# Stream states updated in place in a ring of five rooms, reads of two streams in turn, convolution rows written inside the set-up

## The chip, the core and the metric

One core of a Trainium2 chip runs the whole program. The time is the device time of one execution in microseconds (us), and smaller is better. TensorE (PE) multiplies, VectorE (DVE), ScalarE (ACT) and GpSimd (POOL) compute element by element, SyncE (SP) issues most DMAs. Every engine works through its own list of instructions in order and waits on semaphores.

## What is computed

Two layers, each with a token mixer (layer 0: S5, layer 1: mLSTM) and a convolutional feed-forward net (FFN), run over one prompt of 1024 tokens and over eight running streams of 16 tokens. The change lies at the end of layer 0's FFN and the projection of layer 1 (whose last convolution rows are outputs), and in the mLSTM of the eight streams, which have four heads with a 512 x 512 state matrix each:

```python
num = einsum(sc, v) + a * einsum('bqhk,bhvk->bqhv', q, C)      # read of the old state C
den = sum(sc) + a * einsum('bqhk,bhk->bqh', q, n)
h = num / maximum(abs(den), exp(-m_t))
C_new = decay * C + einsum('blh,blhv,blhk->bhvk', wg, v, k)    # update, an output
n_new = decay * n + einsum('blh,blhk->bhk', wg, k)
xp = concatenate([buf, x]); new_buf = xp[:, -(width - 1):]     # last rows of a convolution, an output
```

All data are float32. Eight streams times four heads are 32 state matrices of 1 MB; each is read once from HBM and written once.

## The kernel before

The program is a row of stages. A stage is a block: each engine runs its part, and the block ends when all five have arrived at its end. `front` ends layer 0 and projects layer 1; it leaves the last convolution rows in two tiles, `tails` (44 tiles of 18 columns) and `m_tails` (16 tiles of 27 columns).

`rows_out` (L1111) then runs twice, once for each tile, as a block of its own: PE turns four tiles at a time into one of four PSUM banks (L1126), DVE copies the bank into `stack` (L1133), SP stores the rows when all are there (L1139) and waits for the store.

`cell_setup` (L2335) makes the masks (POOL, L2374 to L2396), folds the weights and computes the gates' running sums and maxima, most of it in one chain on DVE (L2439 to L2492). ACT serves the chain with four functions (L2425 to L2433), PE with the picking of gate rows at the start (L2410) and turns at the end (L2418).

`mlstm_streams` (L2876) has three blocks. In the first, SP loads (L2945 `nrow`, L2947 `row`, L2951 the inputs x of a head) and each of the four heads is projected (PE, L2515 and L2518), turned into weights, split into a head and a rest (the operands of the updates) and written to HBM by SP (`write`, L2943). POOL loads these back in another layout, 48 rows to a pair of streams: `stack_load` (L2933), 12 DMAs for a head, into `v3` and `k3`, of which there are two each. The order of SP's list is the order in which the lines are written. POOL does the stacking loads of heads 0 and 1 here, those of heads 2 and 3 in the second block.

The second block does the 32 state matrices, one a step, head by head and stream by stream. In a step PE turns the matrix (16 transposes of 128 x 128 into banks 0 to 3, L3100), ACT copies the four banks to `cts` (L3114), PE makes four updates of 128 x 512 into banks 5 and 7 in turn (L3082, contraction over the 48 stacked rows), DVE adds each to the decayed state (L3126), and PE makes four reads (L3088), whose result of 32 rows lies in the PSUM partitions of the stream's pair, `32 * (s // 2)`. A head's first step has one more matmul (L3094). The order of PE's work is written by hand: transposes, two updates, two reads, two updates, two reads. Three rooms of four strips hold states that were loaded (`craw`; the third is made of other tiles), two more (`cnew`) hold new states until they are stored. SP, when a step's updates are done, issues the load for three steps later (L2923 and L2926) and then the store (L3068). DVE waits until the store before last has landed, since it writes into its room.

The third block ends the streams (normaliser, norm, output). After it come the prompt's mLSTM, the down projection and layer 1's FFN, which the change does not touch.

## Time and profile before

| | us |
|---|---|
| median of three timed runs (3935.04 to 3937.03) | 3936.26 |
| time of the profiled execution | 3934.65 |
| its span, first to last instruction | 3932.6 |
| writing out the convolution rows (two blocks) | about 22.7 |
| set-up | 55.5 |
| streams, first block | 64.2 |
| streams, second block (32 steps) | 240.0 |

PE is busy 89% of the span, DVE 49%, ACT 29%, POOL 13%. A timeline row gives the start, the length and the engine, then the line, operation and tiles with the number of instructions merged, and in brackets how long the engine was idle before it and who released it. "SPq" and "POOLq" rows are DMAs being issued, not moved. A float32 matmul appears as two records on PE, except a transpose and one with rounded operands. PEclk is the share of the full PE clock that was granted: 0.50 is 1.2 GHz and 1.00 is 2.4 GHz.

### The profile page before, as it was taken

To read this page: it belongs to the slowest core of one execution; us is meant where nothing else is said; L and a number is where in the kernel's file an instruction comes from. 1 tells how busy PE (TensorE), PEld (TensorE's weight loads), DVE (VectorE), ACT (ScalarE), POOL (GpSimd) and SP (SyncE) were. 2 spreads that over 40 slices of the span, in tenths; PEclk is the share of its full clock that TensorE was granted. 3 is DMA by queue.
4 is the path that set the end of the run, shared out by engine and by line. 5 is a ranking of instruction groups with operands and counts; after the bars stand their busy time and mean duration, and the time that the engine had idled before them with its cause. 6 is when DMAs were issued, how large, how long until landed. Compare 5 with 4: busy or idle time off the path is not lost. (4 is left out here: it accounts for less than half of the span.)

```text
span 3932.6 us, 53760 instructions
## 1 busy us (share of the span) xinstructions
PE 3504.0 (89%) x20489; PEld 3252.7 (83%) x20489; DVE 1917.5 (49%) x2968; ACT 1135.5 (29%) x1865; POOL 509.5 (13%) x765
## 2 busy tenths in 40 slices
PE   5549999999999989999279969997995999999997
PEld 4449989999999989999144468887995999999996
DVE  8933554445445462222533346664655444454455
ACT  5233343332232232222122212222112423322321
POOL 2240111000000120000011032221001100000000
PEclk7669999999999999999589979999997999999998
DMA  3544431111111223332289722221112111111112
GB/s 78 141 119 136 132 96 43 41 41 44 44 43 43 71 87 121 107 105 93 41 233 309 257 77 84 76 76 70 43 64 76 44 44 41 41 44 44 44 38 101
DMA packets 366173, 337.08 MB, mean 86 GB/s; under 512 B 42758, under 2 KB 293894, under 8 KB 365826
## 3 DMA queue, kind: packets, MB, share of 16 engines
q1 hardware_dynamic: 345332, 289.11, 24.1%
q0 software_dynamic: 13456, 37.61, 3.4%
q10 hardware_dynamic: 7176, 7.35, 0.6%
q8 instruction: 157, 2.57, 0.3%
q14 instruction: 52, 0.43, 0.0%
HBM read 231.12 MB, written 100.53 MB: 84 GB/s over the span
## 5 line engine op out<-in xcount | busy, mean ns | idle before, releaser
L1583 PE MATMUL pair<-x_head,w_head 128*128 128x384 f32 x1488 | 506.5, 340 | 54.3 <-DVE w_rest L840 30.9
L1583 PE MATMUL pair<-x_rest,w_head 128*128 128x384 f32 x1488 | 503.5, 338 | 0.0
L1583 PE MATMUL pair<-x_head,w_rest 128*128 128x384 f32 x1488 | 503.0, 338 | 0.0
L840 DVE TENSOR_TENSOR w_rest<-w_raw,w_head 128x1024 fp32r<-128x1024 f32 x228 | 291.5, 1279 | 416.6 <-ACT w_head L836 416.5
L836 ACT ACTIVATE w_head<-w_raw 128x1024 fp32r<-128x1024 f32 x228 | 242.4, 1063 | 688.6 <-PE pair L856 167.0
L1238 PE MATMUL pair<-x_head,w_head 128*128 128x384 f32 x1056 | 354.0, 335 | 10.3 <-DVE w_rest L840 8.2
L1238 PE MATMUL pair<-x_rest,w_head 128*128 128x384 f32 x1056 | 353.5, 335 | 0.0
L1238 PE MATMUL pair<-x_head,w_rest 128*128 128x384 f32 x1056 | 353.4, 335 | 0.0
L1583 PEld LDWEIGHTS pair<-x_head,w_head 128*128 128x128 f32 x1488 | 284.2, 191 | 59.2 <-issue 51.2
L1328 DVE SCALAR_TENSOR_TENSOR cv<-u,par,cv 128x1024 f32<-128x1024 f32 x88 | 112.8, 1281 | 357.7 <-ACT u L1294 357.7
L1583 PEld LDWEIGHTS pair<-x_rest,w_head 128*128 128x128 f32 x1488 | 284.3, 191 | 0.0
L1583 PEld LDWEIGHTS pair<-x_head,w_rest 128*128 128x128 f32 x1488 | 284.1, 191 | 0.0
L1851 DVE SCALAR_TENSOR_TENSOR cv<-u,par,cv 128x1024 f32<-128x1024 f32 x88 | 112.8, 1281 | 341.1 <-ACT u L1792 341.1
L1238 PEld LDWEIGHTS pair<-x_head,w_head 128*128 128x128 f32 x1056 | 198.7, 188 | 11.3 <-issue 9.1
L1238 PEld LDWEIGHTS pair<-x_rest,w_head 128*128 128x128 f32 x1056 | 198.8, 188 | 0.0
L1238 PEld LDWEIGHTS pair<-x_head,w_rest 128*128 128x128 f32 x1056 | 198.8, 188 | 0.0
L1753 PE MATMUL pair<-a_head,w_head 128*128 128x384 f32 x528 | 179.0, 339 | 2.1 <-DVE f L1882 1.0
L1259 PE MATMUL pair<-a_head,w_head 128*128 128x384 f32 x528 | 179.3, 339 | 1.5 <-DVE f L1355 0.4
L1289 ACT ACTIVATE cv<-pair,par 128x384 f32<-128x384 f32 x132 | 88.5, 670 | 314.9 <-PE pair L1238 303.9
L1259 PE MATMUL pair<-a_rest,w_head 128*128 128x384 f32 x528 | 177.5, 336 | 0.0
L1259 PE MATMUL pair<-a_head,w_rest 128*128 128x384 f32 x528 | 177.5, 336 | 0.0
L1753 PE MATMUL pair<-a_head,w_rest 128*128 128x384 f32 x528 | 176.7, 335 | 0.0
(501 smaller groups left out, 6907.8 us busy)
## 6 DMA issues: line engine op xcount, KB each, us to landing
w_raw<-in_ffn_w_up_dram SPq DMA_DIRECT2D x88, 512.0 KB, 3.8
out_dram<-hs SPq DMA_DIRECT2D x64, 512.0 KB, 7.0
w_raw<-in_s_w_glu_dram SPq DMA_DIRECT2D x48, 512.0 KB, 4.0
w_raw<-in_ffn_w_down_dram SPq DMA_DIRECT2D x44, 512.0 KB, 3.7
hs<-in_state_mlstm_C_dram SPq DMA_DIRECT2D x44, 512.0 KB, 5.8
w_raw<-in_mlstm_w_up_dram SPq DMA_DIRECT2D x32, 512.0 KB, 4.5
f<-in_state_mlstm_C_dram SPq DMA_DIRECT2D x40, 256.0 KB
xm_d<-xm SPq DMA_DIRECT2D x16, 576.0 KB, 3.9
```

Source lines behind the costliest of these rows:

```text
L836: act.activation(self.head[slot][:, :], self.raw[slot][:, :], ACT.Copy).then_inc(self.rounded, 1)
L840: dve.tensor_tensor(self.rest[slot][:, :], self.raw[slot][:, :], self.head[slot][:, :].bitcast(F32), ALU.subtract).then_inc(self.split, 1)
L1238: m = pe.matmul(banks[k % 2][c][:, 0:TB], lhs[k % 2][:, P * i:P * i + P], rhs[:, i, TB * c:TB * c + TB], start=(i == 0 and q == 0), stop=( ...
L1259: ins = pe.matmul(banks[m % 2][c][:, 0:TB], lhs[m // 4][:, cols], rhs[s][:, k, TB * c:TB * c + TB], start=(k == 0 and q == 0), stop=(k == ...
L1289: act.activation(cv[g][:, TB * c:TB * c + TB], bk[c][:, 0:TB], ACT.Identity, scale=at(par, t, TAP + H, TAP + H + 1), bias=at(par, t, BIAS, ...
L1328: ins = dve.scalar_tensor_tensor(out=cp, in0=up[:, j:j + SEQ], scalar=tw, in1=cp, op0=ALU.mult, op1=ALU.add)
L1583: m = pe.matmul(out[:, 0:TB], lhs[slot][:, P * k:P * k + P], rhs[:, k, TB * c:TB * c + TB], start=(k == 0 and q == 0), stop=(k == KD - 1 a ...
L1753: ins = pe.matmul(out[:, 0:TB], lhs[m // 4][:, cols], rhs[s][:, k, TB * c:TB * c + TB], start=(k == 0 and q == 0), stop=(k == 1 and q == 2))
L1851: ins = dve.scalar_tensor_tensor(out=cp, in0=up[:, j:j + SEQ], scalar=tw, in1=cp, op0=ALU.mult, op1=ALU.add)
```

## The change

- The two `rows_out` blocks of layer 0 go. `tails` and `m_tails` live on into `cell_setup`, where PE turns them in 15 batches of four into banks 6 and 7, ACT copies each batch into rows of `hs` (not in use yet), and POOL issues the four stores and waits for them.
- First block of the streams: the inputs of head 0 are loaded first and `nrow` last of the early loads; the turn of `nrow` and its copy come after the last head. Five states are loaded ahead, each after a `write`, not three. POOL does the stacking loads of head 0 alone; those of head 1 start with the second block.
- Second block: the streams of a head go in the order 0, 2, 4, 6, 1, 3, 5, 7. DVE writes the new state over the old one, in one of five rooms. SP stores a step's state from its room, then waits for the store of two steps before and loads the state of three steps ahead into that room.
- PE does the reads of two steps together, in turn, after the transposes of the second; the two streams of such a pair lie in different groups of 32 PSUM partitions. The four updates of a step stand together. `cts` exists twice; the second copy is in tiles that hold operands of the writes, so ACT waits for the writes before step 1.
- Two tiles more stay in memory during `front`, and its start address moves by their size.

The diff, cut to what the text speaks of, without its common indent:

```diff
+        for k, (src, tiles, stores) in enumerate(halos):
+            pool.wait_ge(copied, batches.index((k, 0)) + tiles // 4)
+            for dst, r in stores:
+                pool.dma_start(dst, stacks[k][r:r + dst.shape[0], :]).then_inc(halo_out, 16)
+        pool.wait_ge(halo_out, 16 * 4)
...
+        for n, (k, b) in enumerate(batches):
+            src = halos[k][0]
+            rows_ = src.shape[2]
+            if n >= 2:
+                pe.wait_ge(copied, n - 1)
+            for q in range(4):
+                ins = pe.transpose(bank[6 + n % 2][0:rows_, P * q:P * q + P], src[:, 4 * b + q, :], env.ident[:, :])
+            ins.then_inc(halo_turned, 1)
+        pe.wait_ge(copied, len(batches))
...
+        for n, (k, b) in enumerate(batches):
+            act.wait_ge(halo_turned, n + 1)
+            act.activation(stacks[k][:, 4 * P * b:4 * P * b + 4 * P], bank[6 + n % 2][0:halos[k][0].shape[2], :],
+                           ACT.Copy).then_inc(copied, 1)
...
-cnew, cts = [8, 12], 16
-craw = [[strip(4 * b + t) for t in range(HT)] for b in range(2)] + [[flat(t) for t in (*cell.xc, *cell.xm)]]
+ROOMS = 5
+cts = [[strip(16 + k) for k in range(HT)], [flat(t) for t in (*cell.t1, *cell.t2)]]
+craw = [[strip(4 * b + t) for t in range(HT)] for b in range(ROOMS - 1)] + [[flat(t) for t in (*cell.xc, *cell.xm)]]
...
+order = [(h, s) for h in range(HEADS) for s in (0, 2, 4, 6, 1, 3, 5, 7)]
...
-        sp.dma_start(nrow[:, :], n_in[0].rearrange("s h k -> (s h) k")).then_inc(nrow_in, 16)
-        for h in range(HEADS):
-            sp.dma_start(row[:, h, :], rows_d[h, PCH].rearrange("k t -> (k t)").partition_broadcast(P)).then_inc(row_in, 16)
-        for h in range(HEADS):
+        def inputs(h):
             over(sp, projected, h - 1)
             for dst, src in ((cell.xc, xc_d), (cell.xm, xm_d)):
                 sp.dma_start(dst[h % 2][:, :, :], src.rearrange("k p t -> p k t")[:, HT * h:HT * h + HT, last]).then_inc(
                     x_in[h % 2], 16)
-            if h >= 1:
-                c_load(sp, h - 1, h - 1, 0) if h < 3 else None
-            if h >= 2:
-                write(h - 2)
+
+        inputs(0)
+        for h in range(HEADS):
+            sp.dma_start(row[:, h, :], rows_d[h, PCH].rearrange("k t -> (k t)").partition_broadcast(P)).then_inc(row_in, 16)
+        sp.dma_start(nrow[:, :], n_in[0].rearrange("s h k -> (s h) k")).then_inc(nrow_in, 16)
+        inputs(1)
+        inputs(2)
+        write(0)
+        c_load(sp, 0, order[0][1], 0)
+        inputs(3)
+        write(1)
+        c_load(sp, 1, order[1][1], 0)
+        c_load(sp, 2, order[2][1], 0)
         write(2)
         write(3)
-        sp.wait_ge(projected, HEADS)
-        c_load(sp, 2, 2, 0)
+        for n in range(3, ROOMS):
+            c_load(sp, n, order[n][1], 0)
...
-        pe.wait_ge(nrow_in, 16)
-        for k in range(HT):
-            ins = pe.transpose(bank[6][:, SR * k:SR * k + SR], nrow[:, P * k:P * k + P], env.ident[0:SR, 0:SR])
-        ins.then_inc(n_turned, 1)
...
+        pe.wait_ge(nrow_in, 16)
+        for k in range(HT):
+            ins = pe.transpose(bank[6][:, SR * k:SR * k + SR], nrow[:, P * k:P * k + P], env.ident[0:SR, 0:SR])
+        ins.then_inc(n_turned, 1)
...
-            if h >= 2:
-                pool.wait_ge(wrote[h - 2], 64)
+            if h == 2:
+                pool.wait_ge(wrote[0], 64)
                 for n in range(12):
-                    stack_load(pool, h - 2, n)
+                    stack_load(pool, 0, n)
...
-        dve.wait_ge(n_turned, 1)
-        dve.tensor_copy(nt[:, :, :].rearrange("p k r -> p (k r)"), bank[6][:, 0:HT * SR])
...
+        dve.wait_ge(n_turned, 1)
+        dve.tensor_copy(nt[:, :, :].rearrange("p k r -> p (k r)"), bank[6][:, 0:HT * SR])
...
-c_kept = [env.sem(f"c_kept{k}") for k in range(2)]
-order = [(h, s) for h in range(HEADS) for s in range(STREAMS)]
+c_kept = [env.sem(f"c_kept{k}") for k in range(ROOMS)]
...
-        for h in range(2, HEADS):
-            pool.wait_ge(wrote[h % 2], 128)
-            pool.wait_ge(updated, HT * STREAMS * (h - 1))
+        for h in range(1, HEADS):
+            pool.wait_ge(wrote[h % 2], 64 * (h // 2 + 1))
+            if h >= 2:
+                pool.wait_ge(updated, HT * STREAMS * (h - 1))
             for n in range(12):
                 stack_load(pool, h, n)
...
+            b = i % ROOMS
             sp.wait_ge(updated, HT * (i + 1))
-            if i + 3 < SR:
-                nh, ns = order[i + 3]
-                c_load(sp, i % 3, ns, nh)
             for t in range(0, HT, 2):
-                sp.dma_start(c_out[0, s, h, P * t:P * t + 2 * P, :].rearrange("(t p) k -> p t k", p=P),
-                             two_strips(cnew[i % 2] + t)).then_inc(c_kept[i % 2], 16)
-        for p in range(2):
-            sp.wait_ge(c_kept[p], 16 * SR)
+                if b < ROOMS - 1:
+                    sp.dma_start(c_out[0, s, h, P * t:P * t + 2 * P, :].rearrange("(t p) k -> p t k", p=P),
+                                 two_strips(4 * b + t)).then_inc(c_kept[b], 16)
+                else:
+                    for v in (t, t + 1):
+                        sp.dma_start(c_out[0, s, h, P * v:P * v + P, :], craw[b][v]).then_inc(c_kept[b], 16)
+            n = i + ROOMS - 2
+            if i >= 2 and n < SR:
+                sp.wait_ge(c_kept[n % ROOMS], (32 if n % ROOMS < ROOMS - 1 else 64) * (n // ROOMS))
+                c_load(sp, n % ROOMS, order[n][1], order[n][0])
+        for p in range(ROOMS):
+            sp.wait_ge(c_kept[p], (32 if p < ROOMS - 1 else 64) * ((SR - 1 - p) // ROOMS + 1))
...
+        def reads(i, k):
+            h, s = order[i]
+            pair, r = s // 2, s % 2
+            pe.wait_ge(copied, HT * i + k + 1)
+            return pe.matmul(bank[4 + 2 * (h % 2)][32 * pair:32 * pair + 32, :], qz[h][k][:, 64 * pair + 32 * r:64 * pair + 32 * r + 32],
+                             cts[i % 2][k], start=False, stop=(k == HT - 1), skip_group_check=True)
+
         for i, (h, s) in enumerate(order):
-            pair, r, p, num = s // 2, s % 2, i % 2, bank[4 + 2 * (h % 2)]
-
-            def updates(t0):
-                for t in (t0, t0 + 1):
+            pair, r = s // 2, s % 2
+
+            def updates():
+                for t in range(HT):
                     over(pe, updated, HT * i + t - 1)
                     row = slice(64 * r, 64 * r + S3)
                     pe.matmul(bank[5 + 2 * (t % 2)][:, :], v3[h % 2][row, pair, P * t:P * t + P],
                               k3[h % 2][row, pair, :], start=True, stop=True).then_inc(added, 1)
 
-            def reads(k0):
-                for k in (k0, k0 + 1):
-                    pe.wait_ge(copied, HT * i + k + 1)
-                    ins = pe.matmul(num[32 * pair:32 * pair + 32, :], qz[h][k][:, 64 * pair + 32 * r:64 * pair + 32 * r + 32],
-                                    strip(cts + k), start=False, stop=(k == HT - 1), skip_group_check=True)
-                return ins
...
-            pe.wait_ge(c_in[i % 3], (32 if i % 3 < 2 else 64) * (i // 3 + 1))
+            b = i % ROOMS
+            pe.wait_ge(c_in[b], (32 if b < ROOMS - 1 else 64) * (i // ROOMS + 1))
...
-            updates(0)
-            reads(0)
-            updates(2)
-            reads(2).then_inc(inter, 1)
+            if i % 2 == 0:
+                updates()
+            else:
+                for k in range(HT):
+                    for j in (i - 1, i):
+                        ins = reads(j, k)
+                ins.then_inc(inter, 1)
+                updates()
...
+            if i == 1:
+                act.wait_ge(wrote[0], 128)
+                act.wait_ge(wrote[1], 128)
             for k in range(HT):
                 act.wait_ge(turned, HT * i + k + 1)
                 if k == 0:
-                    over(act, inter, i)
-                act.activation(strip(cts + k), bank[k][:, :], ACT.Copy).then_inc(copied, 1)
+                    over(act, inter, i // 2)
+                act.activation(cts[i % 2][k], bank[k][:, :], ACT.Copy).then_inc(copied, 1)
...
-            p = i % 2
-            over(dve, c_kept[p], 32 * (i // 2))
+            room = craw[i % ROOMS]
+            dve.wait_ge(turned, HT * i + HT)
             for t in range(HT):
                 dve.wait_ge(added, HT * i + t + 1)
-                dve.scalar_tensor_tensor(out=strip(cnew[p] + t), in0=craw[i % 3][t],
+                dve.scalar_tensor_tensor(out=room[t], in0=room[t],
...
-        rows_out(env, tails, [(s_fconv[0].rearrange("s h m -> (s h) m"), 0),
-                              (p_fconv[0, 0], STREAMS * (FTAPS - 1))], 2 * FT, (STREAMS + 1) * (FTAPS - 1))
-        rows_out(env, m_tails, [(s_mconv[0].rearrange("s h m -> (s h) m"), 0), (p_mconv[0, 0], STREAMS * MH)],
-                 IT, (STREAMS + 1) * MH)
+        front(env, i, x_head, x_rest, x_res, par, gates, tails, m_tails, xm_d, xc_d, sz_d)
...
+               member, p_m, s_m, hs,
+               ((tails, 2 * FT, [(s_fconv[0].rearrange("s h m -> (s h) m"), 0), (p_fconv[0, 0], STREAMS * (FTAPS - 1))]),
+                (m_tails, IT, [(s_mconv[0].rearrange("s h m -> (s h) m"), 0), (p_mconv[0, 0], STREAMS * MH)])))
+    early.close()
```

PE in the second block. Before, one step from the head's extra matmul on; the `x2` rows are the halves of updates and of reads:

```order
L3094 MATMUL pair<-f,c_sc_331 128x512
L3100 MATMUL pair<-ident,hs 128x128 x16
L3082 MATMUL pair<-k_354,v_352 128x512 x2
L3088 MATMUL pair<-hs 32x512 x2
L3082 MATMUL pair<-k_354,v_352 128x512 x2
L3088 MATMUL pair<-hs 32x512 x2
L3100 MATMUL pair<-ident,hs 128x128 x16
```

Now, two steps; `hs` and `c_t` are the first and the second copy of the turned state:

```order
L3130 MATMUL pair<-f,c_sc_326 128x512
L3137 MATMUL pair<-ident,hs 128x128 x16
L3125 MATMUL pair<-k_349,v_347 128x512 x4
L3137 MATMUL pair<-ident,hs 128x128 x16
L3115 MATMUL pair<-hs 32x512
L3115 MATMUL pair<-c_t_330,hs 32x512
L3115 MATMUL pair<-hs 32x512
L3115 MATMUL pair<-c_t_331,hs 32x512
L3115 MATMUL pair<-hs 32x512
L3115 MATMUL pair<-c_t_332,hs 32x512
L3115 MATMUL pair<-hs 32x512
L3115 MATMUL pair<-c_t_333,hs 32x512
```

The four updates of a step lost the reads between them, and the eight reads of two steps stand in a row, one from each in turn.

SP at the start of the streams' first block, before; the names with `_parts` are the writes of a head:

```order
L2945 DMA nrow<-in_state_mlstm_n_dram 32x512
L2947 DMA row<-rows_d 128x256 x4
L2951 DMA f<-xc_d 128x4x128
L2951 DMA f<-xm_d 128x4x128
L2951 DMA f<-xc_d 128x4x128
L2951 DMA f<-xm_d 128x4x128
L2923 DMA hs<-in_state_mlstm_C_dram 128x2x512 x2
```

And now:

```order
L2972 DMA f<-xc_d 128x4x128
L2972 DMA f<-xm_d 128x4x128
L2977 DMA row<-rows_d 128x256 x4
L2978 DMA nrow<-in_state_mlstm_n_dram 32x512
L2972 DMA f<-xc_d 128x4x128
L2972 DMA f<-xm_d 128x4x128
L2972 DMA f<-xc_d 128x4x128
L2972 DMA f<-xm_d 128x4x128
L2967 DMA v_parts<-c_hn_328 128x512
```

Head 0's inputs passed five DMAs, and no state is loaded before the first write.

ACT in the set-up, now; before, the two rows of L2450 were not there:

```order
L2447 ACTIVATE t_307<-t_306 4x1152
L2450 ACTIVATE hs<-pair 18x512 x11
L2450 ACTIVATE hs<-pair 27x512 x4
L2453 ACT_TABLE_LOAD
L2453 ACTIVATE t_306<-m 4x1152
```

The 15 copies stand between the logarithm and the exponential of the running maxima.

## Rows read from the trace of the kernel before

**Rows 1.** The page's first line.
```profile
span 3932.6 us, 53760 instructions
```
**Rows 2.** Stages: length, busy time (instructions) of five engines, PEclk, DMA share, GB/s.
```profile
1892.00:1947.50 55.50, 10.07 (x30) 3.40 (x30) 39.97 (x41) 9.66 (x8) 3.98 (x17) 0.50 0.09 5
1947.50:2011.70 64.20, 24.39 (x164) 22.82 (x164) 15.68 (x41) 12.47 (x24) 21.43 (x48) 0.71 0.88 206
2011.70:2251.70 240.00, 231.12 (x904) 101.22 (x904) 89.72 (x128) 68.78 (x132) 12.03 (x24) 0.97 0.87 280
```
**Rows 3.** Timeline of PE's first work in both row stages and the set-up.
```profile
1869.26 6.63 PE L1126 MATMUL pair<-ident,tails 128*18 128x128 f32 x44 [3.27 <-PEq L2100]
...
1883.19 3.58 PE L1126 MATMUL pair<-ident,m_tails 128*27 128x128 f32 x16 [7.30 <-PEq L1119]
...
1892.08 7.83 PE L2410 MATMUL pair<-gates,ident 8*4 8x384 f32 x12 [5.30 <-PEq L86]
```
**Rows 4.** Timeline of ACT in the set-up: the exponential after the gap.
```profile
1937.68 1.16 ACT L2431 ACTIVATE t<-m 4x1152 f32<-4x1152 f32 x1 [21.53 <-DVEq L2483]
```
**Rows 5.** Timeline of the streams' first block and the second's first matmul.
```profile
1951.95 0.43 SPq L2951 DMA_DIRECT2D f<-xc_d  x1
...
1957.73 3.78 PE L2515 MATMUL pair<-f,bd 128*128 128x128 f32 x16 [6.01 <-DMA f<-xm_d]
...
1984.44 3.14 POOL L2933 DMA_DIRECT2D v<-v_parts  x6
...
1996.32 1.88 SPq L2926 DMA_DIRECT2D f<-in_state_mlstm_C_dram  x4
...
2011.79 2.05 PE L3094 MATMUL pair<-f,c_sc 128*128 128x512 f32 x2 [20.29 <-PEq L2936]
```
**Rows 6.** Timeline of one step: transposes, updates, DVE, reads, next transposes.
```profile
2042.81 1.97 PE L3100 MATMUL pair<-ident,hs 128*128 128x128 f32 x16
...
2044.70 0.73 PE L3082 MATMUL pair<-k,v 48*128 48x512 f32 x2
2045.31 1.40 DVE L3126 SCALAR_TENSOR_TENSOR hs<-hs,row,pair 128x512 f32<-128x512 f32 x2 [3.06 <-PE pair L3082]
...
2045.36 1.90 PE L3088 MATMUL pair<-hs 128*32 128x512 f32 x4
...
2047.20 0.73 PE L3082 MATMUL pair<-k,v 48*128 48x512 f32 x2
...
2049.69 0.55 PE L3100 MATMUL pair<-ident,f 128*128 128x128 f32 x3
```
**Rows 7.** Groups of instructions in the steps: busy us, mean ns of one record.
```profile
L3088 PE MATMUL pair<-hs 128*32 128x512 f32 x192 | 94.5, 616 | 0.0
```
**Rows 8.** Timeline of the gate matmuls in the stage before (three column groups).
```profile
1478.49 0.83 PE L1998 MATMUL pair<-xc,gs 128*8 128x384 f32 x6
...
1479.14 0.82 PE L1998 MATMUL pair<-xm,gs 128*8 128x384 f32 x6
```
**Rows 9.** Timeline where DVE waited for a store and PE for DVE.
```profile
2083.14 2.74 DVE L3126 SCALAR_TENSOR_TENSOR hs<-hs,row,pair 128x512 f32<-128x512 f32 x4 [5.55 <-DMA out_dram<-hs]
...
2083.94 0.49 PE L3082 MATMUL pair<-k,v 48*128 48x512 f32 x1 [1.34 <-DVE hs L3126]
```
**Rows 10.** Waits in the second block: total us, times, longest.
```profile
DVE hs L3126 <- DMA out_dram<-hs: 27.6, 6, 6.9
```
**Rows 11.** DMA issues of the page: count, KB each, median us to landing.
```profile
out_dram<-hs SPq DMA_DIRECT2D x64, 512.0 KB, 7.0
...
hs<-in_state_mlstm_C_dram SPq DMA_DIRECT2D x44, 512.0 KB, 5.8
```
**Rows 12.** Three stretches of the steps, columns as in rows 2.
```profile
2063.50:2068.50 5.00, 5.00 (x25) 2.64 (x24) 1.51 (x3) 2.06 (x4) 0.00 (x0) 1.00 0.89 238
...
2077.00:2085.00 8.00, 6.50 (x27) 2.86 (x25) 2.44 (x4) 2.06 (x4) 0.00 (x0) 1.00 1.23 316
2087.50:2094.50 7.00, 7.00 (x29) 3.17 (x28) 2.48 (x4) 2.06 (x4) 0.00 (x0) 0.91 1.05 406
```

## What the change does to the time, predicted

> **What bounds the kernel now.** I read the table of stages first, then the order of time inside each stage that the change touches, then the waits. The profiled execution has a span of 3932.6 us [rows 1] and a time of 3934.65 us, 1.6 below the median of the three timed runs (3936.26); the sum is made against 3934.65 and 1.6 is added at the end. The change touches four neighbouring stages [rows 2]: writing out the convolution rows (from 1869.2), the set-up (55.5 us), the streams' first block (64.2 us) and the 32 stream steps (240.0 us); the rest runs as before. In the first, PE turns rows, then the kernel waits for the store, twice: PE's first turn is at 1869.26, the second stage's at 1883.19, the set-up's first PE work at 1892.08 [rows 3]. In the set-up DVE is busy 40.0 of 55.5 us in one chain, ACT idles 21.5 us in one piece [rows 4], and POOL works for 4.0 us. The first block ends when every engine has arrived. PE stands idle 20.3 us before 2011.79, while SP issued its last DMA by 1998.2 and POOL had begun its 24 stacking loads at 1984.44 [rows 5]: POOL's software-made DMAs end the block, (2011.7 - 1984.4)/24 = 1.13 us each. In the stream steps PE sets the pace: 231 of 240 us busy [rows 2], a step every 2049.69 - 2042.81 = 6.88 us [rows 6].
>
> **Convolution rows into the set-up.** Two PE/DVE/SP stages go. From PE's first turn to the set-up's first work is 22.8 us [rows 3]; of that the barrier that ends a phase stays (1 to 2 us, my estimate from the 8.9 us of the shorter stage), so I take 21.5, bounds 20 and 22.8. The work reappears inside the set-up: 60 transposes on PE, 15 copies on ACT, 4 DMAs on POOL's queue. The copies stand between ACT's logarithm and the exponential that starts at 1937.68, where it idles 21.5 us [rows 4]. A copy of 512 columns takes 0.52 us in the stream steps (68.8 us for 132 [rows 2]), a batch of four transposes at the half clock that holds here [rows 2] about 0.9 (3.58 us for 16 in [rows 3]); with two banks in turn 15 batches cost about 14 us, hidden, with 7 to spare. PE has nothing else before 1937.7. POOL's stores start some 3 us before the copies end, and POOL is waited for only at the end of the stage, 17 us after them; a POOL store that took twice the 7.0 us of SP's stores in the steps [rows 11] would still be covered. If this cover fails the cost is at most about 5 us. Cost taken: 0.
>
> **First block.** The loads of x for head 0 move ahead of five others. They were issued at 1951.95, and PE started on them at 1957.73, 5.8 us later [rows 5]; now they are issued at the block's start, 4.4 us earlier, with an emptier queue. DVE's row loads, moved behind two DMAs, land about when before, and their first result is needed only when PE's 6 us of projection is over. I take 5.9 us earlier for the chain of heads (bounds 4 and 6). The n rows' transposes and copy go from the front to the end, about 1 us on PE and DVE beside SP's and POOL's tails: 0. POOL then issues 12 stacking loads, not 24, starting at 1984.4 - 5.9 = 1978.5: 12 x 1.13 = 13.6, so 1992.1, plus 2 us until POOL arrives: 1994.2. SP must have issued its own: the last writes at 1996.3 - 5.9 = 1990.4, then six loads at 0.47 (1.88 for four [rows 5]): 1993.2. The block ends at 1994.3 rather than 2011.7: **17.4 us** (bounds 12 and 19). The other 24 - 12 loads move beside the stream steps, where POOL is free.
>
> **Stream steps on PE.** In a step [rows 6] the transposes take 2044.70 - 2042.81 = 1.89 us, two updates 0.66, two reads 1.84, and these two once more. A read is two records of 512 columns. One lasts 0.62 us [rows 7] and four in a row 1.90 [rows 6], so they start 0.43 apart; four reads are 3.42 us plus two entries of 0.13. Now two streams' eight reads stand together, and neighbours write different groups of 32 PSUM partitions. Does PE overlap them? The gate matmuls do this: three matmuls of 384 columns into three groups, six records, take 0.65 us from start to start [rows 8]. One after another they would take 6 x 0.32 = 1.92 us (0.32 being 384/512 of a read's 0.43). So they overlap fully, and I take 8 x 0.43 + 0.13 = 3.55 us for both streams, against 7.1 before (3.4 to 7.0 are the bounds).
> The Trainium skill, "TensorE: Matmul & The Clock Gate", section "Measured speedup vs the span model", gives 2.38 times for three column tiles; by that our pair would take 3.55 + 0.9 = 4.4 us. The gate rows show 1.92/0.65 = 2.95 times here, so the trace says more overlap than the page does.
>
> The reads no longer fill the time between updates. The four updates now stand together on two banks, and each waits for DVE to empty the one before last. DVE starts 0.61 us after the update (2045.31 against 2044.70) [rows 6] and does one per 0.66; the next update starts 0.80 after DVE's start (2083.14 to 2083.94) [rows 9]. So updates start at 0, 0.34, 1.40, 2.06, and the next work at 2.06 + 0.32 = 2.38 us, against 1.32 before. Per pair of streams: 2 x (1.89 + 2.38) + 3.55 = 12.1 us, before 13.77. Times 16: 220.3 -> 193.9.
>
> The rest of the stage was 240.0 - 220.3 = 19.7 us: four extra matmuls, a cold first step, the end, and stalls where DVE waited for stores of its two output rooms: 27.6 us in six waits [rows 10], of which PE felt only the part beyond its own work; I put 9 us on it (5 to 12). In place, with five rooms, DVE never waits for a store. In their stead a load waits for its room's store of two steps earlier, and SP's later stores queue behind that wait. The store landed in 7.0 us, the load in 5.8 [rows 11]; two steps are 12.1 us, and three steps (18 us) lie between a load's issue and its use, less one step's work: covered. While POOL's 12 loads run (1.57 MB in 14 us) the queues gave 316 GB/s in all [rows 12], and 3 us of slack are short of a deficit of about 5 us, twice: 4 us (0 to 10). The last in-place update ends 1 us later against PE's end: +1. Stage: 193.9 + 19.7 - 9 + 4 + 1 = 209.6, **30.4 us** less.
>
> **DMA.** The steps now move 59 state blocks of 1.05 MB and 36 stacking loads of 0.13 MB: 66.6 MB. A step of 6.06 us asks for 346 GB/s. With a full queue the trace shows 406 over 7 us; a load that leads a queue shows 238 [rows 12]. Now the store goes first, so the load is queued ahead of its turn: 66.6 MB/406 = 164 us, below PE's 194.
> The Trainium skill, "DMA: Bandwidth & Descriptors", section "Specifications", gives a limit of about 358 GB/s per core; by it the 66.6 MB take 186 us, still below PE. The 406 of this trace is above it.
>
> **Sum.** 3934.65 - 21.5 - 17.4 - 30.4 = 3865.4, plus 1.6: **3867 us**.
>
> **Rivals.** (B) DMA sets the pace. For: the stage ran at 280 GB/s mean with a DMA share of 0.87 [rows 2], loads are slow when they lead. Against: 406 when queued. 66.6 MB at 316 is 211 us, at 280 it is 238; with 7 us of start and end the stage is 218 to 245: 3875 to 3902, middle 3886. (C) The reads overlap in part only, because two moving tensors are read at once (the gates' are of one tile): a quarter of the overlap lost is 16 x 0.9 = 14 us: 3881. This is also where the page's 2.38 leads. (D) They do not overlap at all: 16 x 3.4 = 55 us more: 3922. (F) The first block's end is not POOL's; then only the earlier start is left there, and 11 us are missing: 3878. (G) On the other side: SP's wait for a store ahead of the next load closes a ring. A room is busy for load 5.8 + turn and work 7 + store 7.0 = 20 us of the 30 that five steps give. From 30 on it sets the pace. To lose the 69 us each step must be 2.2 us longer, 41 us a turn, so load and store together 34 us and not 12.8: 3945. Only the stretches with POOL's loads come near 30.
>
> **How the numbers follow.** A 0.58, B 0.20, F 0.07, C 0.05, D 0.07, G 0.03. A alone reaches from 3856 (no stalls, block at its better bound) to 3876. To 3896 it takes in C, F and most of B; D and G are left out, 1 in 10, and some of A below and B above. A measurement tells about 0.2% (7.9 us) from no change: faster than 3928.4 is A to D and F, 0.96; same 0.01; slower 0.03.
>
> **What would show it.** Right: PE steps in pairs of 12.1 us, eight reads in 3.55 with starts nearly together; four updates over 2.1 us with waits for DVE; the block before the steps ending 17 us earlier against its start; no idle DVE for stores; the set-up still 55 to 56 us. Wrong: reads 0.43 apart (D), transposes waiting for state loads outside POOL's stretches (B or G), SP held up long on store semaphores (G), ACT's exponential in the set-up later than before.

## Result: 3908.3 us, 0.7% faster, where 3867 was forecast

The changed kernel takes 3908.34 us (median of four runs, 3903.63 to 3911.35), the kernel before 3935.91: a ratio of 0.9927 (95% interval 0.9914 to 0.9940). Forecast were 3867 us and a range of 3856 to 3896. The profiled execution took 3905.37 us; its page begins

```profile
span 3903.4 us, 53745 instructions
```

To see where the time went, the table of stages is read first. Below are the set-up, the streams' first block, and the steps from a head's first extra matmul to the first matmul of the next stage; they answer to [rows 2], and the columns are the same.

```profile
1867.00:1922.30 55.30, 20.91 (x90) 9.03 (x90) 39.97 (x41) 17.83 (x23) 6.09 (x21) 0.56 0.18 16
1922.30:1969.80 47.50, 24.80 (x164) 23.32 (x164) 15.62 (x41) 12.47 (x24) 15.46 (x36) 0.79 0.88 248
1969.87:2221.90 252.03, 210.70 (x905) 116.77 (x905) 88.95 (x133) 74.31 (x132) 18.12 (x36) 0.83 0.89 273
```

In the kernel before, the steps between the same two instructions take 240.87 us (2011.79 to 2252.66). Cut at the same places, the two traces differ like this:

| stretch | before, us | after, us | difference | forecast |
|---|---|---|---|---|
| up to the last gate matmuls | 1865.2 | 1861.3 | -3.8 | 0 |
| from there to the set-up's first matmul | 26.9 | 5.7 | -21.2 | -21.5 |
| set-up and first block, to the first step | 119.7 | 102.8 | -16.9 | -17.4 |
| the 32 steps | 240.9 | 252.0 | **+11.2** | **-30.4** |
| all that follows | 1679.9 | 1681.5 | +1.6 | 0 |

The first and last lines are the scatter of stretches that are the same in both: over the 14 kernels below, the gate matmuls start between 1858.0 and 1863.5, and the last stretch takes 1679 to 1688 us. Two of the three terms came out as forecast. The miss of 41 us lies in the steps, which became slower instead of faster (11.2 + 30.4 = 41.6).

The first two terms read so in the timeline of the changed kernel (start, length, engine, line, tiles, idle before it and releaser):

```profile
1861.33 0.82 PE L1998 MATMUL pair<-xm,gs 128*8 128x384 f32 x6
1867.03 7.83 PE L2419 MATMUL pair<-gates,ident 8*4 8x384 f32 x12 [4.87 <-PEq L86]
...
1899.53 1.07 ACT L2450 ACTIVATE hs<-pair 27x512 f32<-27x512 f32 x2 [0.23 <-PE pair L2428]
1912.63 1.16 ACT L2453 ACTIVATE t<-m 4x1152 f32<-4x1152 f32 x1 [10.73 <-DVEq L2505]
...
1926.98 3.78 PE L2537 MATMUL pair<-f,bd 128*128 128x128 f32 x16 [12.02 <-DMA f<-xm_d]
...
1967.45 1.98 SPq L2950 DMA_DIRECT2D f<-in_state_mlstm_C_dram  x4
...
1969.87 2.04 PE L3130 MATMUL pair<-f,c_sc 128*128 128x512 f32 x2 [8.11 <-PEq L2960]
```

ACT's exponential starts 1912.63 - 1867.03 = 45.60 us into the set-up, to the hundredth as before (1937.68 - 1892.08), with 10.73 us of idle time left ahead of it: the copies are hidden. PE starts on the streams 59.95 us after the set-up's first matmul, not 65.65: 5.7 of the 5.9 us. The first block ends 0.4 us after SP's last DMA was issued (1967.45 + 1.98), and POOL's twelve stacking loads had landed 1.1 us before that, at 1968.3.

Now the steps. This is one pair in the changed kernel; every line is PE's. The reads are single records, two for each matmul; of the eight couples of records (one of each stream) the first and the last stand here.

```profile
2081.73 1.97 PE L3137 MATMUL pair<-ident,f 128*128 128x128 f32 x16
2083.62 0.73 PE L3125 MATMUL pair<-k,v 48*128 48x512 f32 x2
2085.03 0.50 PE L3125 MATMUL pair<-k,v 48*128 48x512 f32 x1 [0.68 <-DVE f L3170]
2085.69 0.49 PE L3125 MATMUL pair<-k,v 48*128 48x512 f32 x1 [0.16 <-DVE f L3170]
2086.11 3.12 PE L3137 MATMUL pair<-ident,hs 128*128 128x128 f32 x16
2089.16 1.06 PE L3115 MATMUL pair<-hs 128*32 128x512 f32 x1
2089.17 1.06 PE L3115 MATMUL pair<-c_t,hs 128*32 128x512 f32 x1
...
2092.66 0.59 PE L3115 MATMUL pair<-hs 128*32 128x512 f32 x1
2092.66 0.59 PE L3115 MATMUL pair<-c_t,hs 128*32 128x512 f32 x1
2093.19 0.73 PE L3125 MATMUL pair<-k,v 48*128 48x512 f32 x2
2094.60 0.50 PE L3125 MATMUL pair<-k,v 48*128 48x512 f32 x1 [0.68 <-DVE hs L3170]
```

Two things are to be seen. The reads of two streams start within 10 ns of each other: they overlap fully. And the first turn takes 1.89 us up to the next work, the second 3.05. The table of the same stretches gives the reason (seventh number: PEclk):

```profile
2081.73:2083.62 1.89, 1.89 (x17) 1.73 (x16) 0.86 (x2) 1.20 (x3) 0.00 (x0) 1.00 0.08 30
2083.62:2086.11 2.49, 1.65 (x5) 0.66 (x5) 1.88 (x3) 0.87 (x2) 0.00 (x0) 1.00 1.03 366
2086.11:2089.16 3.05, 3.05 (x17) 2.72 (x16) 0.86 (x2) 1.79 (x3) 0.00 (x0) 0.60 0.99 267
2089.16:2093.19 4.03, 4.03 (x18) 0.94 (x17) 0.00 (x0) 0.60 (x1) 0.00 (x0) 0.88 1.05 400
2093.19:2095.68 2.49, 1.65 (x6) 0.66 (x5) 1.88 (x3) 0.60 (x1) 0.00 (x0) 1.00 0.83 312
```

After a block of updates in which PE waited for DVE (0.68 and 0.16 us), its granted clock goes from 2.4 to 1.2 GHz, the turn (the sixteen transposes of a step) and the first reads run at half speed, and within the reads the full clock is back. Over the steps PEclk is 0.83, where it was 0.97 [rows 2]; in 20 of 32 steps the sixteen transposes take over 2 us from the first start to the last, against one step before. What PE waited for in the steps (line, releaser, total us, times, longest; the waits for DVE stand between the updates, those for a DMA are for states):

```profile
PE pair L3125 <- DVE hs L3170: 21.1, 50, 0.7
...
PE pair L3137 <- DMA hs<-in_state_mlstm_C_dram: 7.3, 3, 4.6
...
PE pair L3125 <- DVE f L3170: 5.0, 12, 0.7
PE pair L3137 <- DMA f<-in_state_mlstm_C_dram: 1.4, 1, 1.4
```

### The profile page after: what moved, and what is told of

Read it like the earlier page. It is cut to its first block and busy times, and to the rows that moved or that the text cites. A ratio compares the mean times of both kernels' runs of the same rounds, so it can differ in the third digit from the quotient of the medians.

```text
span 3903.4 us, 53745 instructions
## 1 busy us (share of the span) xinstructions
PE 3481.6 (89%) x20489; PEld 3262.9 (84%) x20489; DVE 1908.1 (49%) x2953; ACT 1149.8 (29%) x1880; POOL 511.1 (13%) x769
## 3 DMA queue, kind: packets, MB, share of 16 engines
q1 hardware_dynamic: 345318, 288.49, 24.1%
## 5 line engine op out<-in xcount | busy, mean ns | idle before, releaser
L1583 PE MATMUL pair<-x_head,w_head 128*128 128x384 f32 x1488 | 505.6, 340 | 53.0 <-DVE w_rest L840 30.4
```

What stands on the lines that cost most here:

```text
L1583: m = pe.matmul(out[:, 0:TB], lhs[slot][:, P * k:P * k + P], rhs[:, k, TB * c:TB * c + TB], start=(k == 0 and q == 0), stop=(k == KD - 1 a ...
```

## Experiments

Fourteen more kernels were timed, in four groups, each next to runs of the kernel before, whose medians were 3932.7 to 3936.9 us. A ratio is to the kernel before of the same group, so small differences between kernels are better read from ratios than from medians. "Steps" is the same stretch as above in the profiled execution, PEclk and DMA (share, GB/s) are those of that stretch, and "slow turns" counts the steps whose sixteen transposes take over 2 us (not counted where updates stand between the transposes). Where an expectation says "T0 to T31", it means the time from the first transpose of the first step to that of the last, a shorter stretch: 227.0 us before and 234.1 us in the changed kernel.

| kernel | median us | ratio to before (95%) | steps us | PEclk | DMA | slow turns |
|---|---|---|---|---|---|---|
| before | 3935.91 | | 240.9 | 0.97 | 0.86, 279 | 1 |
| changed | 3908.34 | 0.9927 (0.9914 to 0.9940) | 252.0 | 0.83 | 0.89, 273 | 20 |
| steps_only | 3946.56 | 1.0024 (1.0013 to 1.0036) | 253.0 | 0.83 | 0.83, 265 | 19 |
| alone | 3894.59 | 0.9900 (0.9884 to 0.9917) | 240.8 | 0.97 | 0.94, 284 | 2 |
| fill | 3896.30 | 0.9908 (0.9892 to 0.9925) | 235.1 | 0.94 | 0.95, 292 | 6 |
| nostore | 3894.83 | 0.9901 (0.9885 to 0.9918) | 238.2 | 0.85 | 0.59, 148 | 17 |
| spstack | 3892.80 | 0.9892 (0.9875 to 0.9908) | 239.9 | 0.84 | 0.86, 284 | 19 |
| fill_sp | 3888.38 | 0.9875 (0.9858 to 0.9891) | 234.0 | 0.91 | 0.87, 295 | 9 |
| after_early | 3896.91 | 0.9898 (0.9882 to 0.9915) | 244.2 | 0.83 | 0.91, 280 | 19 |
| fill_early | 3890.56 | 0.9888 (0.9871 to 0.9904) | 228.1 | 0.93 | 0.95, 300 | 6 |
| among | 3933.06 | 1.0001 (0.9991 to 1.0010) | 274.6 | 0.78 | 0.82, 250 | |
| early | 3880.03 | 0.9857 (0.9841 to 0.9874) | 224.9 | 0.91 | 0.99, 304 | |
| early_sp | 3876.96 | 0.9850 (0.9833 to 0.9866) | 226.7 | 0.88 | 0.93, 302 | |
| all_sp | 3873.62 | 0.9845 (0.9827 to 0.9863) | 221.8 | 0.92 | 0.96, 319 | |
| woven | 3897.37 | 0.9902 (0.9885 to 0.9919) | 244.7 | 0.89 | 0.86, 289 | 6 |
| woven4 | 3869.06 | 0.9832 (0.9816 to 0.9849) | 213.2 | 0.94 | 0.98, 327 | 5 |

From the gate matmuls to the first step all of them are within 1 us of the changed kernel, but for steps_only (as before) and all_sp, woven and woven4, which have head 0's stacking loads on SP.

### Is it the clock? fill

Theory: the gaps between the updates cost the clock. Rival: states set the pace, and slow transposes only fill a wait. The filling is left out in the first two steps of each head, and where it begins PE has one wait more, for the bank into which it writes:

```diff
                         for t in range(HT):
+                            if t >= 2 and i % STREAMS >= 2:
+                                for _ in range(6 if t == 2 else 3):
+                                    pe.transpose(bank[6 - 2 * (h % 2)][:, 0:P], env.ident[:, :], env.ident[:, :])
                             over(pe, updated, HT * i + t - 1)
...
+                    if i % STREAMS == 2:
+                        over(pe, kept, h)
```

> The changed kernel with nine transposes of the identity more in a step (six after its second update, three after its third), written to a PSUM bank that nothing reads, where PE otherwise waits for DVE; in three of four pairs of steps. It only adds work to PE. Theory 1, the clock: the gaps between the updates cost PE its clock, so transposes at the half clock (25 us over 32 steps) and reads (7.5 us over 16 pairs) are the loss. With the gaps filled the granted clock of the steps goes from 0.83 to 0.93 or more, most transposes take 1.9 us, and the time falls by 18 to 30 us, to 3878 to 3890. Theory 2, state loads set the pace and slow transposes only fill a wait: PE then waits longer for loads, and the time stays within 6 us of the changed kernel's 3908. If the added work matters itself, the time rises by up to 1 us a step.

More work on PE made the steps 17 us shorter. The work in the gaps reads so (L3125 is the filling), and the turn behind it is quick:

```profile
2087.36 0.73 PE L3128 MATMUL pair<-k,v 48*128 48x512 f32 x2
2088.03 0.87 PE L3125 MATMUL pair<-ident 128*128 128x128 f32 x6
2088.83 0.49 PE L3128 MATMUL pair<-k,v 48*128 48x512 f32 x1
2089.25 0.55 PE L3125 MATMUL pair<-ident 128*128 128x128 f32 x3
2089.73 0.50 PE L3128 MATMUL pair<-k,v 48*128 48x512 f32 x1
2090.16 1.13 PE L3133 MATMUL pair<-hs,sc 128*128 128x512 f32 x2
2091.12 1.91 PE L3142 MATMUL pair<-ident,hs 128*128 128x128 f32 x16
```

Its sixteen turns in the later pairs of a head (steps 4 to 7, 12 to 15, 20 to 23 and 28 to 31) are all quick; in the changed kernel nine of them were slow. The six that are left are steps 0, 1, 2, 10, 11 and 18, in the pair of a head that has no filling or the one right behind it. Three of these, 10, 11 and 18, also stand behind waits for a state, so this run alone can't say which of the two slowed them:

```profile
PE pair L3142 <- issue: 8.6, 2, 4.3
...
PE pair L3142 <- DMA hs<-in_state_mlstm_C_dram: 0.9, 1, 0.9
```

The profile names no releaser for the two of 4.3 us, but the state loads issued at 2032.1 and 2092.9 landed at 2046.9 and 2107.7, 0.1 us before PE went on; it was not the wait for the bank. The kernel's time fell by 12 us (0.9908 against 0.9927) and not by the 18 or more that I expected at least: the filling costs 0.3 us a step (a pair takes 12.95 us, where one with no drop of the clock takes 12.28), the first pair of each head was left as it was, and some 5 us of the 17 are lost in stretches that the edit does not touch. The rival that slow transposes cost nothing is out.

### Is it the DMA engines? nostore

> The changed kernel without the stores of the new states but for one strip of the last (half of the bytes that the steps move), and without the waits for them. Theory 1: only the waits of PE for a state load go, 10 us in five places, and the transposes still run at the half clock in the same steps: 3895 to 3901, granted clock of the steps still below 0.88. Theory 2, loads and stores set the pace: with half the bytes the steps run at PE's 12.3 us a pair, 35 to 40 us less: 3868 to 3875.

This kernel leaves out the stores of the new states, so these are missing from its outputs; it serves only to take bytes off the DMA engines. Its time, 3894.8 us, is at the lower edge of the first case. With half of the bytes and a DMA share of 0.59, the steps take 238.2 us, and 17 turns are slow, as this pair shows although no DMA held it up:

```profile
2001.11 0.73 PE L3118 MATMUL pair<-k,v 48*128 48x512 f32 x2
2002.52 0.49 PE L3118 MATMUL pair<-k,v 48*128 48x512 f32 x1 [0.68 <-DVE f L3163]
2003.17 0.50 PE L3118 MATMUL pair<-k,v 48*128 48x512 f32 x1 [0.17 <-DVE f L3163]
2003.60 3.17 PE L3130 MATMUL pair<-ident,hs 128*128 128x128 f32 x16
```

So the half clock does not hang on the transfers. Taking half of them away gained 14 us: 5.4 of the 8.7 us of PE's waits for states, 5.7 us in turns and reads, of which a few more ran at the full clock, and the rest mostly at the end of the stage.

### Which part of the change does it? alone and steps_only

```diff
-                    if i % 2 == 0:
-                        updates()
-                    else:
-                        for k in range(HT):
-                            for j in (i - 1, i):
-                                ins = reads(j, k)
-                        ins.then_inc(inter, 1)
-                        updates()
+                    updates((0, 1))
+                    reads(i, 0)
+                    reads(i, 1)
+                    updates((2, 3))
+                    reads(i, 2)
+                    reads(i, 3).then_inc(inter, 1)
```

> The changed kernel with the order of work on PE in a step as it was before (two updates, two reads, two updates, two reads), so without reads of two streams in turn; ring of five rooms, order of streams, loads and stores as changed. Theory 1: the reads fill PE's time between updates and the clock stays at 0.95 or more; a pair of steps takes 13.8 us and the waits for stores are gone: the stage takes 232 to 240 us against 252, 3888 to 3897. So the reads in turn would have lost time. Theory 2, the new ring and its loads are what slows the steps: the stage stays over 248 us, 3904 or later.

It is as expected: 3894.6 us, and the steps take 240.8 us, at the upper end of the first case, with PEclk 0.97. That has two consequences. The reads in turn cost 11 us net, since without them the changed kernel is faster. And the ring of five rooms, with the twelve stacking loads more that now run beside the steps, brought nothing: 240.8 against 240.9 before. DVE no longer waits for a store, but PE now waits for states while POOL's stacking loads run:

```profile
PE pair L3137 <- DMA hs<-in_state_mlstm_C_dram: 4.8, 2, 3.3
PE pair L3137 <- DMA f<-in_state_mlstm_C_dram: 0.9, 1, 0.9
```

The other way round, steps_only is the kernel before with the new second block alone:

> The kernel before with the new second block alone (states in place in five rooms, order of streams, reads in turn, SP's stores and loads); the convolution rows are written in their own two blocks, the inputs and POOL's stacking loads of heads 0 and 1 stand in the first block as before. In the changed kernel the second block took 11 us longer than before, by PE's half clock and its waits for states, not less. If the three parts add up, this kernel is slower than before: 3945 to 3950, less the waits that POOL's loads of head 1 cost at its start (up to 5 us): 3940 to 3950. If the steps were only slow because the stages ahead of them were short (stacking loads of head 1, an earlier start), it is faster than before: 3900 to 3925.

3946.6 us, slower than before by 0.24%, and steps of 253.0 us, 12 more than before. It is the first case: the parts add up, and the second block is a loss wherever it stands.

### The second cause: spstack, fill_sp, after_early, fill_early

Beside the clock, PE waits for states. In a stretch with POOL's stacking loads and in one without, the table of stretches of the changed kernel shows (last two: DMA share, GB/s):

```profile
2036.00:2050.00 14.00, 9.98 (x40) 4.42 (x40) 5.49 (x8) 2.40 (x5) 2.46 (x5) 0.85 1.27 216
2054.00:2062.00 8.00, 7.16 (x24) 4.25 (x25) 2.81 (x4) 2.63 (x5) 0.00 (x0) 0.50 1.05 406
```

The DMA engines are full in both, and move 216 GB/s in one and 406 in the other. (The share adds up the times of all packets and can pass 1.) In the first stretch the stacking loads' packets took 57% of the engines' time for 1.36 MB and those of SP's queue, which are states, 70% for 1.65 MB: a megabyte of either held the engines 5.9 us, and 2.6 us in the second. So a megabyte of stacking loads is dear, and one of states beside them is as dear. A stacking load of 128 KB goes into 16 partitions, a state load of 512 KB into 128.

In `spstack` POOL's loads of heads 1 to 3 are gone, and SP issues them behind its loads, two a step; each head's loads get a semaphore of their own:

```diff
+                    g = h + 1
+                    if g < HEADS and i % STREAMS < 6:
+                        if i % STREAMS == 0:
+                            sp.wait_ge(wrote[g % 2], 64 * (g // 2 + 1))
+                        for m in (2 * (i % STREAMS), 2 * (i % STREAMS) + 1):
+                            stack_load(sp, g, m)
```

> The changed kernel with the stacking loads of heads 1, 2 and 3 issued by SP, two behind each of the first six steps of the head before, instead of twelve in a row by POOL. Theory 1: POOL's stacking loads take 1.1 us each of the DMA engines for 128 KB, one after another, and hold the state loads up; that is what PE's waits for states at steps 2, 9, 10, 18 and 19 are (10 us beyond the usual). They go, the half clock stays: 10 us less than the changed kernel on the same chip, T0 to T31 from 234 to 222 to 226 us. Theory 2: the waits come from SP's own wait for a store ahead of a load: with 36 more DMAs in SP's queue they stay or grow, 0 to 5 us more.

12 us less in the steps (239.9), with PEclk still 0.84 and 19 slow turns; PE's waits for states fell from 8.7 to 0.2 us. POOL's bursts do cost their share. Then both edits together:

> The changed kernel with both single edits: the nine filling transposes a step, and the stacking loads of heads 1 to 3 by SP, two a step. If the half clock and POOL's stacking loads are two causes beside each other, both gains add: T0 to T31 is 234 - 16 - 12 = 206 us, 203 to 209, and no pair of steps is over 15 us. If one only makes room for the other, it stays at 214 us or more.

This was a miss: 234.0 us, no better than fill alone (235.1), and 217.3 from T0 to T31. The two gains do not add, but not because loads came late again:

```profile
PE pair L3139 <- DMA hs<-in_state_mlstm_C_dram: 1.2, 3, 0.7
```

PE's waits for states fell from 9.6 us in fill to 1.2 here. What went the other way is the clock: nine turns are slow instead of six, PEclk is 0.91 instead of 0.94, and PE is busy for 219.6 us where fill was for 212.3, with the same instructions. These nine are steps 0 to 3, 9, 10, 18, 26 and 27, again all in the unfilled first pair of a head or the pair behind it, and none of them stands behind a wait for a state; the turns behind the three waits are quick. That separates what fill left open: the gaps do it without a late state.

Late loads were to be tried on their own as well, with the load of a state moved ahead of the wait for the updates:

```diff
+                    n = i + ROOMS - 2
+                    if i >= 2 and n < SR:
+                        sp.wait_ge(c_kept[n % ROOMS], (32 if n % ROOMS < ROOMS - 1 else 64) * (n // ROOMS))
+                        c_load(sp, n % ROOMS, order[n][1], order[n][0])
                     sp.wait_ge(updated, HT * (i + 1))
...
-                    n = i + ROOMS - 2
-                    if i >= 2 and n < SR:
-                        sp.wait_ge(c_kept[n % ROOMS], (32 if n % ROOMS < ROOMS - 1 else 64) * (n // ROOMS))
-                        c_load(sp, n % ROOMS, order[n][1], order[n][0])
```

> The changed kernel, and SP issues the load of the state of three steps ahead before it waits for a step's updates, not behind its store. The half clock on PE is left as it is. If PE's waits for states in the changed kernel (10 us in five places) come from loads that are issued too late, the steps get 5 to 15 us shorter, 237 to 247 us against 252, with the transposes at the half clock as often as before. If PE's waits themselves set off the half clock, more goes: 225 to 237 us. If the waits come from POOL's stacking loads alone, nothing changes: 250 to 254 us.

244.2 us, 8 less, with 19 slow turns and 2.2 us of waits for states: it is the first case. Late loads are part of the second cause, and nearly as many turns are slow without them, so PE's waits for states are not what sets off most of the half clock. With the filling:

> The changed kernel with the nine filling transposes a step and SP's loads issued before the updates are waited for. If the half clock and late loads are the two things that separate the changed kernel from my 12.1 us a pair, most pairs take 12.3 to 13.0 us and the steps 215 to 224 us, against 252 in the changed kernel and 235 with the filling alone. If the DMA engines are full with POOL's 36 stacking loads in any order, they stay at 228 to 235 us.

228.1 us, where full DMA engines were to keep it. But PE waits 0.3 us for states in all, so they are not the reason. Most pairs take 12.3 to 13.0 us now, and two take 17.6: steps 2 and 3 and steps 18 and 19, right behind an unfilled pair, with turns and filling at the half clock. All six slow turns lie there or in the first pair. Filling in the first pairs too was not tried. The median, 3890.6 us, lies 10 us over the fastest of its runs (3879.84), whose like the profile shows; between runs this kernel scatters more than the others.

### Updates without gaps: among, early, early_sp, all_sp

If gaps are the trouble, the updates can stand between other work. An update needs no turned state, so those of step i can go among the transposes of step i + 1:

```diff
                         ins.then_inc(turned, 1)
+                        if i >= 1:
+                            update(i - 1, k)
```

> The changed kernel with each of a step's four updates placed behind a batch of four transposes of the next step. No work is added or taken away. A batch and an update are 0.43 + 0.34 = 0.77 us, above DVE's 0.66 an update, so PE has no gap. Theory 1, the clock and the gaps: a pair of steps costs PE 2 x 3.1 + 3.55 = 9.8 us instead of 14 to 16, the granted clock stays over 0.95, and DMA or PE sets the pace, at 66.6 MB / 400 GB/s = 167 us at best; with 15 us of start and end the stage takes 180 to 205 us, so 3908 - 252 + 180 to 205 = 3836 to 3861. Theory 2, loads behind a wait for a store set the pace at 280 GB/s mean: the stage stays at 238 us or more, 3894 or later.

This one failed: 3933 us, and steps of 274.6 us with

```profile
PE pair L3136 <- DMA hs<-in_state_mlstm_C_dram: 23.5, 10, 10.0
```

PE has next to no gap in its updates, but a step's store and the load behind it are issued a step's turn later, and PE waits 13 times for a state, 28.7 us in all; 13 turns with their updates take over 4 us where 3.4 is usual (PEclk 0.78). The edit of the loads was made for this kernel first:

> The kernel with the updates among the next step's transposes, with SP's load of the state of three steps ahead issued before SP waits for the step's updates instead of behind its store. Stacking loads by POOL as changed. If the ring (a load issued only after updates, behind two stores) is what holds that kernel at 16 us a pair, T0 to T31 falls from 252 to 205 to 225 us, the time by 25 to 45 us. If the DMA engines themselves are full (share 0.95), it falls by less than 10 us.

224.9 us, 50 less, and 206.5 from T0 to T31, in the first case. A pair takes 11.7 us where nothing is late. Here the ring was the cause, and the DMA share rose from 0.82 to 0.99. On top of it, SP issues the stacking loads of three heads (early_sp) and of all four (all_sp):

> Both edits on the kernel with the updates among the transposes: loads before the updates are waited for, and stacking loads by SP, two a step. If ring and POOL's stacking loads are the two causes, the DMA queue stays full at about 400 GB/s, T0 to T31 is 170 to 190 us and the time 50 us or more below the changed kernel. If the loads set the pace at the 280 GB/s that the steps had before, T0 to T31 stays at 225 us or more.

> The kernel before this one in the list, and also head 0's stacking loads by SP in the first block (12 x 0.47 = 5.6 us of its queue, where it waits for the third head), the fourth state's load ahead of the last write, and the fifth's at the start of the second block. The first block should then end when SP has issued the last write, at about 1966 against 1969.4: 3 us less. If SP's queue delays the writes or the inputs instead, it is slower by up to 4 us.

early_sp is no better than early in the steps (226.7 against 224.9; T0 to T31 208.2, where I had 170 to 190 or 225 and more). The waits for DMAs changed, though, in early and then in early_sp:

```profile
PE pair L3136 <- DMA f<-in_state_mlstm_C_dram: 9.4, 1, 9.4
...
PE pair L3136 <- DMA hs<-in_state_mlstm_C_dram: 7.7, 1, 7.7
```

```profile
PE pair L3133 <- DMA hs<-in_state_mlstm_C_dram: 5.7, 4, 2.0
PE pair L3133 <- DMA k<-k_parts: 2.2, 1, 2.2
```

Two long waits became five short ones, 7.9 us instead of 17.1, while PE was busy for 211.5 us instead of 200.6, at PEclk 0.88 instead of 0.91. A wait of 7.7 us made its pair of steps 12.4 us longer (24.1 against 11.7), and one of 2.0 us still 7.3 (19.0). The six waits over 1 us in the two kernels each cost 3 to 7.5 us beside their length, by turns and reads at the half clock, the short ones as much as the long ones.

all_sp brings the 3 us: from the first projection to the first step 38.6 us instead of 43.4.

### Updates among the reads: woven, woven4

woven is all_sp with the updates of a pair moved from the transposes to the reads, and with the stacking loads spread over all eight steps of a head:

```diff
-                        if i >= 1:
-                            update(i - 1, k)
                     if i % 2 == 1:
                         for k in range(HT):
                             for j in (i - 1, i):
                                 ins = reads(j, k)
                             if k == HT - 1:
                                 ins.then_inc(inter, 1)
+                            for t in (2 * k % HT, 2 * k % HT + 1):
+                                update(i - 1 + k // 2, t)
```

> The last kernel of the second list (all stacking loads by SP, loads before the updates are waited for) with the eight updates of a pair of steps placed among its eight reads, two behind every two reads, and the stacking loads spread over all eight steps of a head. PE's work in a pair is 2 x 1.9 + 8 x 0.43 + 8 x 0.34 = 10.0 us instead of 11.7 and without a gap. If PE sets the pace, T0 to T31 falls from 203 to 165 to 175 us. If the DMA engines do (62 MB at 400 GB/s and 36 stacking loads of about 1.1 us each: 155 + 40 = 195 us), it stays between 190 and 203 us, with PE waiting for states and its clock falling at the waits.

Both cases missed: 244.7 us. PE's pair takes 10.6 us, where 10.0 was worked out, but the steps' waits are

```profile
PE pair L3132 <- DMA k<-k_parts: 40.3, 3, 14.0
```

I had spread the stacking loads to the last step of a head, behind stores and loads, and PE stood at the start of each new head. woven4 issues them three a step in the first four steps:

> The kernel with a pair's updates among its reads, with the stacking loads by SP three a step in the first four steps of a head, not over all eight. There PE waited about 14 us at the start of each new head for the stacked rows. If only these waits made it slow, the steps fall from 245 to 195 to 212 us and it is the fastest. If 36 stacking loads of about 1.1 us and 62 MB at 400 GB/s fill the DMA engines, the wait moves to the middle of a head and the steps take 215 to 225 us, as with the updates among the transposes (222).

213.2 us, between the two cases, and 3869.06 us: a ratio of 0.9832 (0.9816 to 0.9849) to the kernel before, the fastest here. One stretch and its waits:

```profile
1969.97:2183.20 213.23, 184.03 (x905) 95.31 (x905) 90.94 (x133) 69.10 (x132) 0.00 (x0) 0.94 0.98 327
...
PE pair L3132 <- DMA hs<-in_state_mlstm_C_dram: 21.6, 7, 5.5
```

The DMA share is 0.98 over the whole stretch. PE's work would be 16 x 10.6 = 170 us; it waits 22.5 us for states. Of its five slow turns one is the very first and the other four stand right behind waits of 3.6 to 5.5 us; with no gaps between updates there is no other. That the transfers now set the pace is read from these rows; no run took them away here.

## Why the prediction was wrong, step by step

- **Convolution rows, -21.5:** right, -21.2, and the cover held (10.7 us of ACT's idle time left, 7 forecast).
- **First block, -17.4:** right, -16.9, with 5.7 us from the earlier inputs. The end was close between POOL and SP; it was SP's.
- **Reads, 3.55 us for eight:** right in its mechanism. They overlap fully, start within 10 ns, and take 3.56 us where PEclk is 1.00. Partial or no overlap (C, D) did not happen.
- **Updates, 2.38 us a block:** 2.49, because the next work starts 0.42 us behind the last update and not 0.32; 32 x 0.11 = 3.5 us more. The waits for DVE stood there as worked out. Some blocks ran at the half clock in part, 1.9 us more.
- **The step that failed** is the one that I never wrote: the durations 1.89 (turn) and 3.55 (reads) were taken from a stage with PEclk 0.97, while the prediction itself put waits for DVE into every block of updates (26.1 us in the trace, 21.1 + 5.0). I counted the gaps and not what PE's clock would do behind them. From start to the next work, the 32 turns take 86.1 us in the changed kernel against 32 x 1.89 = 60.5, and the 16 blocks of reads 64.3 against 16 x 3.55 = 56.8: 25.6 + 7.5 = **33 us** of the miss. fill, fill_sp and nostore show it as a cause of its own. It would have turned the sign of the stage: -30.4 + 33 = +3. In [rows 2] both levels stood side by side: PEclk 0.97 in a stage that is 96% busy, 0.71 in one that is not.
- **Stacking loads beside the steps, 4 us (0 to 10):** 8.7 us of waits for states, and 12 us with spstack. I had set 1.57 MB against 316 GB/s, as if their bytes counted; but the engines are busy and move 216 GB/s. The time that [rows 5] showed in the first block (1.13 us each) was the nearer one: in the steps of the changed kernel the landings of a burst lie 0.9 to 1.4 us apart.
- **Stalls for stores, -9:** nothing gained in the end. alone has no such stall and the same steps as before: PE's own waits for states took their place.
- **DMA, 164 us below PE's 194:** too low by the same error. woven4, with the share at 0.98, takes 213 us for the stage.
- **Rival B** (transfers set the pace, 3886) does not explain the miss, since nostore keeps 17 slow turns; with PE freed from its gaps, in woven4, it is what seems to be left. **Rival G** (the ring closed by SP's waits) did not decide here, but it did in among, where the order of loads is worth 50 us.
- **"What would show it"** named the turns only as waiting for loads. Four of them did wait, 8.7 us in all; twenty ran slowly. PEclk stood in no line of it.

I had forecast 209.6 us for the stage, and 252.0 were measured. Clock, updates, their slow blocks, and waits beyond the 4 us forecast make 33.1 + 3.5 + 1.9 + 4.7 = 43.2 against these 42.4 us; the rest of the stage (extra matmuls and the end, 11.2 us) was about 1 us less than forecast. Two slips in the prediction do not matter: 16 pairs of 12.1 are 193.4 and not 193.9, and rival G's 69 us give 3936 and not 3945.

What stays open: why some turns behind the same gaps are quick (12 of 32) and others not; no run here varied it. That is also why no run shows what fewer gaps, and not none, would give. Nor was it tried to bring the stacked rows in with fewer or wider transfers, which is where I would look for the next gain.

## What to carry to other kernels

When work that filled PE's waits is moved away, the waits have two prices: their own length, and the clock of what comes behind. So a sum may use a duration only with the PEclk at which it was measured, and has to ask at which one it will run. When a wait goes, look at PE's busy time too: in fill_sp and early_sp the clock took back what the shorter waits gave. And of a DMA the time for which it holds the engines counts, not its bytes: the stacking loads here landed 0.9 to 1.4 us apart beside the steps, about what a state load of four times the size takes (1.29 us at 406 GB/s). In a ring of rooms, a load should be issued when its room is free, not when a step happens to end.

## What the hardware showed

Granted clock: in the pair shown above PE went from 2.4 to 1.2 GHz behind a block of updates with waits of 0.68 and 0.16 us, and in nostore as well, where no transfer held it up. 20 of 32 turns ran slowly in the changed kernel. With work in the gaps of all but the first pair of a head, 21 turns were slow in three kernels together (fill, fill_sp, fill_early), all of them in such a first pair or the pair behind it. The Trainium skill, "TensorE: Matmul & The Clock Gate", section "Loop structure matters more than you think", gives two cases: a good one, in which DVE copies out of PSUM while PE's next matmuls follow at once, and a bad one, in which PE waits long for a DMA. The changed kernel is neither: PE waits for DVE, at most 0.7 us at a time, and its clock fell all the same.

Overlap: two M=32 matmuls of 512 columns with different moving tensors, into two groups of 32 PSUM partitions, start within 10 ns and take no longer than one (0.59 us a record, eight reads in 3.56 us at PEclk 1.00).

Transfers: stacking loads of 128 KB into 16 partitions took 1.13 us each in [rows 5], and landed 0.9 to 1.4 us apart in the steps of the changed kernel, where 512 KB take 1.29 us at 406 GB/s. A stretch with many of them ran at 216 GB/s with a DMA share of 1.27, and the states' bytes cost more time in it as well. Spread over the steps by SP instead of in bursts by POOL they took 12 us off the changed kernel's steps (spstack), and nothing off early's (early_sp). That the small number of partitions is the reason was not separated from their small size.
